# Values of the prompt heads mixed per head by key blocks, exponentials three units ahead, and another order of the memory score groups

## What is computed

```python
# 1) latent attention of the prompt, 4 heads, causal
s = (q_lat @ c^T + q_rope @ k_rope^T) * MLA_SCALE      # mla_scores
s = where(kpos <= qpos, s, -inf)
p = softmax(s, -1)
o = p @ c                                              # then times w_uv, into w_out
# 2) the same for the samples, against 8 pages of cached latents each
# 3) cross-attention into 256 memory tokens, 4 heads of 256
mk, mv = (m @ w_mk), (m @ w_mv)                        # prompt; the samples have cached mk, mv
s = q @ mk^T * MEM_SCALE;  p = softmax(s);  o = p @ mv
# 4) SwiGLU, final norm
```

## Time and profile before

| | us |
|---|---|
| median of 3 runs | 903.75 (900.0 to 905.21) |
| the profiled execution | 899.05 |
| its span, first to last instruction | 897.3 |
| prompt heads, first score to last low part | 135.6 to 183.2 |
| memory stage, TensorE idle or at half clock, mostly | 372 to 391 |

### The profile page before, as it was taken

The page is one execution under the profiler, slowest core; times in us unless marked ns, Lnnn a source line. Parts: engine busy times, 40 slices in busy tenths (PEclk is TensorE's granted clock), DMA queues, the critical chain, the costliest instruction groups (busy, mean ns, idle before and its releaser), DMA issues.

```text
span 897.3 us, 16200 instructions
## 1 busy us (share of the span) xinstructions
PE 828.3 (92%) x6599; PEld 788.0 (88%) x6599; DVE 484.9 (54%) x1055; ACT 327.2 (36%) x714; POOL 103.1 (11%) x143
## 2 busy tenths in 40 slices
PE   5989989877899999789999899999999999999994
PEld 4979978733799998689799899999999999999994
DVE  5577556584354457665555475555555555222322
ACT  5314676510342323355533343333333333112312
POOL 0366104020134000000035100000000000000000
PEclk8999998879799999889999999999999999999998
DMA  7412337040723714573623233333332232332312
GB/s 218 122 48 81 87 96 293 2 175 1 257 71 101 253 48 142 207 258 115 219 72 95 71 94 95 94 95 95 95 92 86 87 91 88 109 110 83 88 42 95
DMA packets 133792, 102.57 MB, mean 114 GB/s; under 512 B 8567, under 2 KB 127280, under 8 KB 130639
## 3 DMA queue, kind: packets, MB, share of 16 engines
q1 hardware_dynamic: 128231, 87.17, 31.7%
q0 software_dynamic: 1792, 10.49, 3.0%
q10 hardware_dynamic: 3696, 3.88, 1.3%
HBM read 96.59 MB, written 5.17 MB: 113 GB/s over the span
## 4 chain that ended last, share of the span: by engine, by line
PE 77%; DVE 6%; ACT 4%; DMA 3%; issue 2%; SPq 0%; ACTq 0%; DVEq 0%
PE ps L1944 23%; PE ps L1946 23%; PE ps L1945 23%; DMA wraw<-in_w_mk_dram 2%; DVE turned_c L1667 1%; PE ps L2281 1%; PE ps L2421 1%; DVE prod L1738 1%; DMA kv_slot<-in_cache_mem_v_dram 1%; PE ps L2376 1%; PE ps L2377 1%; PE ps L2378 1%; PE ps L2329 1%; DVE turned_r L1668 1%; PE ps L2253 0%
## 5 line engine op out<-in xcount | busy, mean ns | idle before, releaser
L1944 PE MATMUL ps<-B_hi,whi 128*128 128x260 f32 x992 | 283.4, 286 | 9.9 <-DVE wlo L1394 4.3
L1946 PE MATMUL ps<-B_hi,wlo 128*128 128x260 f32 x992 | 281.4, 284 | 0.0
L1945 PE MATMUL ps<-B_lo,whi 128*128 128x260 f32 x992 | 281.2, 283 | 0.0
L1394 DVE TENSOR_TENSOR wlo<-wraw,whi 128x512 fp32r<-128x512 f32 (+1 forms) x250 | 170.2, 723 | 167.1 <-ACT whi L912 164.8
L912 ACT ACTIVATE whi<-wraw 128x512 fp32r<-128x512 f32 (+1 forms) x250 | 140.3, 610 | 201.8 <-PE ps L1946 159.2
L1944 PEld LDWEIGHTS ps<-B_hi,whi 128*128 128x128 f32 x992 | 187.9, 189 | 11.9 <-issue 9.3
L1946 PEld LDWEIGHTS ps<-B_hi,wlo 128*128 128x128 f32 x992 | 188.3, 190 | 0.0
L1945 PEld LDWEIGHTS ps<-B_lo,whi 128*128 128x128 f32 x992 | 188.1, 190 | 0.1
L1945 PE MATMUL ps<-h_lo,whi 128*128 128x260 f32 x352 | 99.7, 283 | 0.0
L1946 PE MATMUL ps<-h_hi,wlo 128*128 128x260 f32 x352 | 99.4, 282 | 0.0
L1944 PE MATMUL ps<-h_hi,whi 128*128 128x260 f32 x352 | 99.4, 282 | 0.0
(11 more groups left out here) (405 smaller groups left out, 1286.4 us busy)
## 6 DMA issues: line engine op xcount, KB each, us to landing
wraw<-in_w_gate_dram SPq DMA_DIRECT2D x22, 512.0 KB, 3.8
wraw<-in_w_up_dram SPq DMA_DIRECT2D x22, 512.0 KB, 3.8
kv_slot<-in_cache_mem_k_dram SPq DMA_DIRECT2D x8, 1024.0 KB, 9.3
kv_slot<-in_cache_mem_v_dram SPq DMA_DIRECT2D x8, 1024.0 KB, 6.9
wraw<-in_w_down_dram SPq DMA_DIRECT2D x16, 512.0 KB, 4.0
wraw<-in_w_in_dram SPq DMA_DIRECT2D x9, 512.0 KB, 4.1
wraw<-in_w_out_dram SPq DMA_DIRECT2D x8, 512.0 KB, 4.1
wraw<-in_w_xq_dram SPq DMA_DIRECT2D x8, 512.0 KB, 5.2
```

What stands on the lines that cost most here:

```text
L1394: return dve.tensor_tensor(dst, src, high.bitcast(F32), ALU.subtract)
L1944: pe.matmul(dst, left[0], right[0], start=first, stop=False)
L1945: pe.matmul(dst, left[0], right[1], start=False, stop=False)
L1946: return pe.matmul(dst, left[1], right[0], start=False, stop=last)
```

## The change

In the prompt heads, maxima and exponentials run three units ahead and scores four. The turned probabilities of a whole head are kept (two buffers, in turn, of ten 128-column rows ordered by key block), and `values(h)` multiplies a whole head at once: key block 0 with 512 queries, block 1 with 384, block 2 with 256, block 3 with 128, three matmuls each. It is issued after the first unit of the next head. For i = 3 the high and the low part are two operations each. The buffers take the place of the one in which the past of sample 4 was gathered early; the gathers of samples 4 to 7 now wait for the last values. In the memory stage, groups 5 to 7 are put together anew, so that the keys of samples 3 and 4 are used up after group 5 and those of 5 and 6 after group 6, samples 4 and 5 swap key slots, and the value loads are issued two weight tiles earlier, behind waits for group 5 (after tile 4), 6 (after tile 6), 7 and 8.

```diff
 SPREADS = [...
-           [[(1, 3), (1, 4)], [(1, 5), (1, 6)]], [[(2, 3), (2, 4)], [(2, 5), (2, 6)]],
-           [[(3, 0), (3, 1)], [(3, 2)]], [[(3, 3), (3, 4)], [(3, 5), (3, 6)]],
+           [[(1, 3), (1, 4)], [(1, 5), (1, 6)]], [[(2, 3), (2, 4)], [(3, 3), (3, 4)]],
+           [[(2, 5), (2, 6)], [(3, 5), (3, 6)]], [[(3, 0), (3, 1)], [(3, 2)]],
            [[(0, 7), (1, 7)], [(2, 7), (3, 7)]]]
-K_SLOT, V_SLOT = [0, 1, 2, 3, 4, 5, 6, 7], [3, 5, 4, 6, 2, 7, 2, 7]
+K_SLOT, V_SLOT = [0, 1, 2, 3, 5, 4, 6, 7], [3, 5, 4, 6, 2, 7, 2, 7]
...
-        PT_at = [o_cq + i * (i + 1) // 2 * P * 4 for i in range(5)]
-        PT_hi = [at(f"PT_hi{i}", [i + 1, P], F32R, PT_at[i]) for i in range(4)]
-        PT_lo = [at(f"PT_lo{i}", [i + 1, P], F32R, PT_at[4] - o_cq + PT_at[i]) for i in range(4)]
+        PB = 10 * P * 4
+        PT_hi = [at(f"PT_hi{i}", [10, P], F32R, o) for i, o in enumerate((o_wuk, o_rstd))]
+        PT_lo = [at(f"PT_lo{i}", [10, P], F32R, o_wuk + PB * (i + 1)) for i in range(2)]
...
-        c_at = [g0, g0 + CB, o_ol, o_b3, o_rstd, o_cq, o_ring, o_ring + CB]
+        c_at = [g0, g0 + CB, o_ol, o_b3, o_cq, o_ring, o_ring + CB, o_rstd]
...
+        PT_ROW = [(0, 4), (4, 7), (8, 10), (7, 8)]
+        def pt_parts(i):
+            cut = [(0, min(i + 1, 3), slice(i, i + 3 * min(i, 2) + 1, 3))]
+            return cut + [(3, 4, slice(7, 8))] if i == 3 else cut
...
             for i in range(2, len(MEM_TILES) + 2):
                 load_w(S_MEM + i)
-                if i == 5:
-                    freed(sp, ("qb", 7, 1))
-                if 5 <= i < 9:
-                    load_kv(NB + i - 5)
-                if i == 10:
-                    load_kv(NB + 4)
-                    freed(sp, ("qb", 8, 1))
-                if i == 11:
-                    load_kv(NB + 5)
+                if i in (4, 6, 8, 9):
+                    freed(sp, ("qb", {4: 5, 6: 6, 8: 7, 9: 8}[i], 1))
+                for b in {4: (0,), 5: (1,), 6: (2,), 7: (3,), 9: (4,), 10: (5,)}.get(i, ()):
+                    load_kv(NB + b)
...
-                elif b == 5:
+                elif b == 4:
                     gp.wait_ge(pv_done, NH)
+                elif b == 7:
+                    gp.wait_ge(val, VAL["turned", 1] + 1)
...
             exps(0)
             exps(1)
+            exps(2)
...
-                high(("pt", h, i), PT_hi[i][:, :, :], b[:, 0:(i + 1) * P].rearrange("p (j q) -> p j q", j=i + 1))
-                if n + 2 < len(us):
-                    exps(n + 2)
-                if i == 0 and h:
+                turned = b[:, 0:(i + 1) * P].rearrange("p (j q) -> p j q", j=i + 1)
+                *most, (j0, j1, rows) = pt_parts(i)
+                for k0, k1, r in most:
+                    act.activation(PT_hi[h % 2][:, r, :], turned[:, k0:k1, :], ACT.Copy)
+                high(("pt", h, i), PT_hi[h % 2][:, rows, :], turned[:, j0:j1, :])
+                if n + 3 < len(us):
+                    exps(n + 3)
+                if i == 1 and h:
                     attended(h - 1)
...
-            def values(n):
-                h, i = us[n]
-                split(("pt", h, i))
-                if i == 0 and h:
+            def values(h):
+                split(("pt", h, 3))
+                if h:
                     split(("pv", h - 1))
-                q = slice(i * P, (i + 1) * P)
-                for j in range(i + 1):
-                    ins = mm3(accO[:, q], (v_hi[:, j, h * P:(h + 1) * P], v_lo[:, j, h * P:(h + 1) * P]),
-                              (PT_hi[i][:, j, :], PT_lo[i][:, j, :]), j == 0, j == i)
-                if i == 3:
-                    ins.then_inc(pv_done, 1)
+                p_hi, p_lo = PT_hi[h % 2], PT_lo[h % 2]
+                v = [(v_hi[:, j, h * P:(h + 1) * P], v_lo[:, j, h * P:(h + 1) * P]) for j in range(4)]
+                rows = [(p_hi[:, k0:k1, :], p_lo[:, k0:k1, :]) for k0, k1 in PT_ROW]
+                pe.matmul(accO, v[0][0], rows[0][0], start=True, stop=False)
+                for j in (1, 2, 3):
+                    mm3(accO[:, j * P:TP], v[j], rows[j], False, False)
+                pe.matmul(accO, v[0][0], rows[0][1], start=False, stop=False)
+                pe.matmul(accO, v[0][1], rows[0][0], start=False, stop=True).then_inc(pv_done, 1)
...
-                if n + 3 < len(us):
-                    scores(*us[n + 3])
-                if n:
-                    values(n - 1)
-            values(len(us) - 1)
+                if n + 4 < len(us):
+                    scores(*us[n + 4])
+                if i == 0 and h:
+                    values(h - 1)
+            values(NH - 1)
```

More of the change, by code:

```diff
@@ L133, in bank_order @@
     us = units()
-    o += [("s",) + u for u in us[0:3]] + [("snew",)]
+    o += [("s",) + u for u in us[0:4]] + [("snew",)]
     for n in range(len(us)):
         o += [("pt",) + us[n]]
-        if n + 3 < len(us):
-            o += [("s",) + us[n + 3]]
+        if n + 4 < len(us):
+            o += [("s",) + us[n + 4]]
     o += [("own",)] + [("sc", b) for b in range(NB)] + [("ot",), ("uvs",)]
@@ L200, in val_order @@
     us = units()
-    o += [("negm",) + us[0], ("negm",) + us[1], ("rs",) + us[0]]
+    o += [("negm",) + us[0], ("negm",) + us[1], ("negm",) + us[2], ("rs",) + us[0]]
     for n in range(len(us)):
-        o += [("rs",) + v for v in us[n + 1:n + 2]] + [("negm",) + v for v in us[n + 2:n + 3]]
+        o += [("rs",) + v for v in us[n + 1:n + 2]] + [("negm",) + v for v in us[n + 3:n + 4]]
     o += [("turned", b) for b in range(NB)] + [("bias",), ("own_p",), ("spread_p",), ("rows",)]
@@ L419, in build @@
         take(2 * RPB)
-        c_at = [g0, g0 + CB, o_ol, o_b3, o_rstd, o_cq, o_ring, o_ring + CB]
-        r_at = [g0 + 2 * CB, o_wuk, o_wuk + RPB, o_pool, o_pool + RPB, o_cq + CB, o_cq + CB + RPB, o_ring + 2 * CB]
+        c_at = [g0, g0 + CB, o_ol, o_b3, o_cq, o_ring, o_ring + CB, o_rstd]
+        r_at = [g0 + 2 * CB, o_rstd + PB, o_pool + RPB, o_pool, o_cq + CB, o_cq + CB + RPB, o_ring + 2 * CB, o_wuk]
         past_c = [at(f"past_c{b}", [TPP, KVL], F32, c_at[b]) for b in range(NB)]
@@ L1250, in value_tile @@
                 if h == 0:
-                    freed(act, ("qb", 6, 1))
+                    freed(act, ("qb", 7, 1))
                 else:
@@ L1635, in _ @@
             maxes(1)
+            maxes(2)
             normalise(0)
@@ L1639, in _ @@
                     normalise(n + 1)
-                if n + 2 < len(us):
-                    maxes(n + 2)
+                if n + 3 < len(us):
+                    maxes(n + 3)
                 b = full(dve, ("pt", h, i))
-                low(("pt", h, i), PT_lo[i][:, :, :], b[:, 0:(i + 1) * P].rearrange("p (j q) -> p j q", j=i + 1), PT_hi[i][:, :, :])
-                if i == 0 and h:
+                turned = b[:, 0:(i + 1) * P].rearrange("p (j q) -> p j q", j=i + 1)
+                *most, (j0, j1, rows) = pt_parts(i)
+                dve.wait_ge(hi, SPLIT["pt", h, i] + 1)
+                for k0, k1, r in most:
+                    rest(PT_lo[h % 2][:, r, :], turned[:, k0:k1, :], PT_hi[h % 2][:, r, :])
+                low(("pt", h, i), PT_lo[h % 2][:, rows, :], turned[:, j0:j1, :], PT_hi[h % 2][:, rows, :])
+                if i == 1 and h:
                     attended(h - 1)
@@ L2218, in _ @@
             scores(*us[2])
+            scores(*us[3])
             after(("sprod",))
```

1 line of the change is left out of this document (removed).

## The result

| us | before | after |
|---|---|---|
| median | 904.44 (900.0 to 905.21, 4 runs) | 891.88 (888.98 to 895.61, 4 runs) |
| profiled execution | 899.05 | 891.84 |
| its span | 897.3 | 889.9 |

The changed kernel takes 0.9876 of the time before, 95% interval 0.9834 to 0.9918: 11.2 us by this ratio, 12.6 between the medians, where 7.3 were forecast. Between the two profiled executions it is 7.2 us, since that of before lies 5.4 us under its median. A second set of runs gave 0.9865 (0.9832 to 0.9899). One thing in the account of the change is to be set right: the value loads are issued one weight tile earlier, not two (the first now follows tile 4, before it followed tile 5).

A forecast was written before the change was run, and what follows sets the result against it. TensorE, busy 92% of the span, leaves time only where it idles, runs at half clock or does removable work. Heads -1.8, gathers 0 and memory stage -5.5 give 891.7 against the profiled execution, 896.4 as median; range 889.5 to 904.

The forecast's parts named there:

- A head, 9.0 forecast: Prompt heads: with exponentials three ahead a head takes about 9.0 us instead of 9.86, -0.9; bounds 7.1 and 9.9.
- the hand walk: Prompt heads: both queues followed over one head in the new order, giving VectorE waits of 2.0 to 2.1 us, not 2.9.
- Merged values: Prompt heads: values by key block cut TensorE's work by 1.4 us a head, called not the gain since TensorE idles already.
- Ramp +0.7, tail -0.7: Ends of the heads stage: fourth unit's scores ahead of the first turning cost +0.7; one last values block gives about -0.7.
- Sum of the heads, -1.8: Prompt heads: +0.7 - 2 x 0.9 - 0.7 = -1.8 us, between +0.7 and -8.
- Gathers, 0: Past stage: sample 4's later gather is hidden by VectorE's turning, cost 0; sample 7 needs its gather 11 us after issue.
- Memory stage, -5.5: Memory stage: diagonal's matmul 4.2 us earlier and 1.3 from the clock behind it, -5.5 us, from -1 to -8.
- TensorE as the bound of the heads: Prompt heads: a head falls to 6.6 to 7.1 us, heads gain some 7, total 891.2; chance 0.12.
- The memory stage gives nothing: Memory stage: tile 5 late or waiting only moved, so only the heads' 1.8 us remain, 902; chance 0.20.
- The slower rival: Heads 1 to 3: waits of about 1.7 us drop TensorE's clock, 904.6, or 909.2 with the memory stage; chance 0.08.
- the rival's 4.6 us: Memory stage: clock falls in two new waits, 48 value-tile matmuls cost 0.21 instead of 0.12 each, 4.6 us more; chance half of 0.08.

The follow-up runs named there:

- exps_two: The changed kernel with maxima and exponentials two units ahead again, scores still four ahead and values merged; ratio to before 0.9915.
- ahead_only: The kernel before with the new memory stage and, in its heads, only the look-ahead changed, values per unit as before; ratio to before 0.992.
- narrow: The changed kernel with each head's values at the same place but made by 30 matmuls of 128 columns instead of 12 wide ones; ratio to before 0.9986.
- gathers_later: The changed kernel with the first four samples' gathers waiting until head 0's values are mixed; ratio to before 0.9887.
- all_moves: The changed kernel with the first sample turned before the last A_lo, tile 5 issued before the first value loads, and later gathers; 884.15 us, ratio to before 0.9851.
- heads_only: The changed kernel with the memory stage of before, so only the new heads and gathers; 894.36 us, ratio to before 0.997.
- memory_only: The kernel before with only the new score groups, key slots and load order of the memory stage; 891.12 us, ratio to before 0.9936.
- tile5_first: The changed kernel with weight tile 5 issued before the wait for group 5 and the first two value loads after it; 889.66 us, ratio to before 0.985.
- early_turn: The changed kernel with VectorE turning the first sample of the past before it takes the last A_lo; 887.52 us, ratio to before 0.982.
- after_again: The changed kernel unaltered, run again in a second set; 892.23 us, ratio to before 0.9865.

## Why the prediction was right, point by point

The time, 891.88 us, lies in the range; it is 4.5 us below the predicted 896.4. The profiled execution came at 891.84 where 891.7 was worked out. That closeness is luck: a stop of 2.4 us and a past stage longer by 2.1 us, which the sum did not have, cancel larger gains in the heads and the memory stage.

- **A head, 9.0 forecast:** 8.79 and 8.81. VectorE's waits are 0.98, 0.48 and, before the low part of the 384-column unit, 0.50, together 1.96; the hand walk had 2.0 to 2.1. The waits for exponentials went, as said.
- **Merged values are "not the gain":** right in the sum, wrong in the reason. Merging alone gave 0.25 us in the one clean period of exps_two, the look-ahead 0.8 on top; the one clean period with the look-ahead and no merging was the shortest of all, 8.53 (ahead_only). But "TensorE has idle time already" did not make its work free: in narrow 1.05 of 1.4 us came out. The walk had the block on the chain, the sentence on idle time forgot it.
- **Ramp +0.7, tail -0.7:** the ramp came as forecast where it can be seen. The first turning starts 5.6 us after the first score (140.48 - 134.89) where before took 4.9 (140.49 - 135.62). Up to the second turning of head 1 before took 15.6 us. The same heads without a stop took 16.3 and 15.9 where TensorE began at half clock for a part (gathers_later, all_moves) and 15.4 where it began at full clock (heads_only); the changed kernel took 17.7, with its stop. The tail, from the last second turning to the turning behind the last A_lo, gained 1.4 us (12.1 to 10.7), in heads_only 0.9. In sum the heads without a stop gave 2.9 to 3.6 us, more than forecast; with it 1.4.
- **Sum of the heads, -1.8:** 2.7 us in the runs of heads_only, with an interval of 0.8 to 4.6. In the first pair of traces it was taken back in the past stage, about half by the clock and half by the late going-on of VectorE and ScalarE; the prediction had neither term.
- **Gathers, 0:** no wait of VectorE for a gather in any of the timelines read. There was more room than the prediction reckoned: sample 7 was turned at 201.8, 14.4 us after its gather was issued (187.36), not 11.
- **Memory stage, -5.5:** 6.7 between the first two traces, 5.7 (3.7 to 7.8) in the runs of memory_only. With the new order the two stretches around the diagonal take 83.8 to 84.3 us in every trace (tile5_first and its kin 81.3 to 81.5); with the old one 90.6, 91.1 and, in heads_only, 88.8, so it is the old order whose loss varies. Issue of tile 5, its 6.2 us to first use, the wait of 2.49 for it and the diagonal at 380.94 (380.9 forecast) came as worked out. Mis-sized was the clock behind the diagonal: 2.5 us instead of 1.3, since the full difference came, not half. TensorE's new waits were 2.3 us, not 4, and the half clock behind them did not reach the diagonal.
- **The rivals.** TensorE as the bound of the heads (7 us less) did not come; TensorE's part of it did, in narrow. "The memory stage gives nothing" falls with memory_only. The slower rival: the clock held in the changed kernel from 150 to 174 (1.00, and waits of 1.31 did not bring it down), so the heads did not pay. But its mechanism is real. In exps_two, with waits of 1.95 us, the clock fell inside head 2. In the memory stage the half clock did come behind the two new waits, as the rival said (0.76 and 0.67 from 364 to 376), and cost nothing, because VectorE's queue set the diagonal; the rival's 4.6 us there took for granted that TensorE's work sets the time. What the Trainium skill (TensorE: Matmul & The Clock Gate, "HAM oscillation — how this bites in real kernels") warns of, waits between bursts that bring the half clock back, fits the past stage (0.50 from 186 to 189, behind a wait of 4.17 us) and the memory stage, not the heads of the changed kernel.

**Open.** The halves apart give 2.7 + 5.7 = 8.4 us; the whole gave 0.9876 and 0.9865, 11 to 12 us. With intervals of about 4 us on each side this can be chance. If it is not: the two halves ran in a set where the kernel before takes 897 us, the whole in sets where it takes 904, and where before loses these 7 us was not seen: the one trace of it from such a set is that of an execution at 899.05. Nor is it settled what makes the stops, and whether merging adds anything once the look-ahead is there.

## What to carry to other kernels

An engine's idle share doesn't tell what its work costs: ask where the work stands in the chain that goes round once per iteration. In a block moved into one lump on that chain three quarters of any added length came out (narrow), and merging it into wider operations is what made the lump bearable; left spread over the head, the same work may have cost less (ahead_only, one period). When a load is moved forward in a queue, look at the loads it passes: putting the one weight tile that is needed next ahead of them gave 2.5 us more. And a wait that no reordering shortens can still be filled, as the turning of the first sample did (3.0 us of the past stage, 4.7 between the medians). And the engine that a row names as the releaser is not always the cause: lay the same rows of a sister kernel beside it.

## What was not expected of the hardware

- In the first runs and in one of the three later sets VectorE and ScalarE went on late after TensorE. In the changed kernel the last matmul of the scores of unit (1, 1) ended at 144.43, the maximum, which besides waits only for VectorE's own earlier work, began at 147.36, 2.9 us later; ScalarE's high part of a turning that ended at 144.75 began at 147.41. TensorE itself went on meanwhile. In early_turn it came again: scores ended at 185.54, ScalarE went on at 188.39 and VectorE at 188.47. The small one at 190.6 in the changed kernel, one us, is also in after_again and tile5_first. In all these places the gathers hold the DMA share at about 1.0 (about 390 to 430 GB/s); but the same traffic passed without a stop in all traces of the first and the third set and in that of before. What causes it is open.
- Work at half clock that starts 2.1 us earlier did not bring the full clock earlier in this pair: it was back between 189 and 192 in both kernels, although the scores began at 183.99 and 186.14. It is no rule: in tile5_first they began at 182.81, and the clock was back sooner (0.60 from 186 to 189, 1.00 from 189 to 192).
- The stretch from o_rows to the first wlo took 5.5 to 5.8 or 7.4 to 7.8 us, never between, in fourteen traces with the same instructions there. It is TensorE's clock. The first two rows are of before, the others of exps_two. Each pair spans 20 steps of the same row of matmuls of 8 columns, so they start 0.21 us apart in the one trace and 0.11 in the other:

```profile
224.05 0.36 PE L1944 MATMUL ps<-ols_hi,whi 128*128 128x8 f32 x1
228.31 0.35 PE L1946 MATMUL ps<-ols_hi,wlo 128*128 128x8 f32 x1
...
222.31 0.25 PE L1956 MATMUL ps<-ols_hi,whi 128*128 128x8 f32 x1
224.54 0.25 PE L1958 MATMUL ps<-ols_hi,wlo 128*128 128x8 f32 x1
```

Two traces of nearly the same kernel can so differ by 2 us in a stretch that no edit touches, by where the fall of the clock lands.
